# Sample chunks of two token mixers in column and row tiles, placed by 0/1 matrices, with four weight blocks moved between state updates

## The reference, cut to what matters

```python
def gdn_chunk(S, inp):            # S: (B, H, dk, dv)
    ...
    v_new = value - jnp.einsum('bhld,bhdv->bhlv', kcd, S)
    o = jnp.einsum('bhld,bhdv->bhlv', q * jnp.exp(G)[..., None], S) + jnp.einsum('bhtj,bhjv->bhtv', qk, v_new)
    S_new = S * jnp.exp(GL)[..., None] + jnp.einsum('bhjd,bhjv->bhdv', k * jnp.exp(GL - G)[..., None], v_new)
def gla_chunk(S, inp):
    ...
    o = jnp.einsum('bhtc,bhcv->bhtv', q * jnp.exp(Bc), S) + jnp.einsum('bhtj,bhjv->bhtv', A, v)
    S_new = S * jnp.swapaxes(jnp.exp(BL), -1, -2) + jnp.einsum('bhjc,bhjv->bhcv', k * jnp.exp(BL - Bc), v)
```

## Time and profile before

| | us |
|---|---|
| median of 3 runs (lowest, highest) | 993.27 (988.12, 995.01) |
| the profiled execution, its own time | 989.5 |
| its span, first to last instruction | 987.8 |
| chunk 2 of stage two from its first product with old states (267.83) to the start of stage three's blocks (344.22) | 76.4 |
| blocks 0 to 7 of stage three, to the last copy's start (379.96) | 35.7 |
| chunk 2 of stage three, first update (452.12) to the end of its outputs (487.43) | 35.3 |

### The profile page before, as it was taken

One profiled execution on the slowest core, in us unless ns is written; L12 is line 12 of the kernel. 1 busy time (PEld: TensorE's weight loads), 2 busy tenths in 40 slices (PEclk: granted clock), 3 DMA queues, 4 the chain that ended last, 5 costly groups with the idle time before them and its releaser, 6 DMA issues. The chain is left out here.

```text
span 987.8 us, 16585 instructions
## 1 busy us (share of the span) xinstructions
PE 911.3 (92%) x7010; PEld 775.9 (79%) x7010; DVE 421.3 (43%) x714; ACT 296.8 (30%) x595; POOL 222.2 (22%) x242
## 2 busy tenths in 40 slices
PE   8999989997999699999978999999899999999993
PEld 7988868886998589868848999999898666665551
DVE  5787854445313533053165643167234222222223
ACT  6775553230112325131036544423211000000003
POOL 8411326554241000000043400575400000000000
PEclk9999999997697699997559999999989999999998
DMA  9934024000002494401066455444059999999992
GB/s 241 291 98 127 1 54 131 1 1 1 2 1 86 137 311 129 128 10 43 1 215 182 131 169 170 143 157 159 13 175 375 423 422 420 421 421 418 422 410 65
DMA packets 97895, 175.41 MB, mean 178 GB/s; under 512 B 9012, under 2 KB 84372, under 8 KB 85477
## 3 DMA queue, kind: packets, MB, share of 16 engines
q1 hardware_dynamic: 97816, 174.29, 49.4%
HBM read 163.13 MB, written 10.95 MB: 176 GB/s over the span
## 5 line engine op out<-in xcount | busy, mean ns | idle before, releaser
L272 PE MATMUL ps<-rounded,rounded 128*128 128x304 f32 x632 | 197.3, 312 | 13.5 <-DVE rounded L260 9.5
L274 PE MATMUL ps<-rounded,rounded 128*128 128x304 f32 x632 | 192.6, 305 | 0.0
L273 PE MATMUL ps<-hL,rounded 128*128 128x304 f32 x504 | 153.9, 305 | 0.0
L272 PEld LDWEIGHTS ps<-rounded,rounded 128*128 128x128 f32 x632 | 120.8, 191 | 24.9 <-DVE rounded L260 9.7
L274 PEld LDWEIGHTS ps<-rounded,rounded 128*128 128x128 f32 x632 | 120.9, 191 | 0.0
L260 DVE TENSOR_TENSOR rounded<-ring,rounded 128x2048 fp32r<-128x2048 f32 x36 | 83.8, 2328 | 71.5 <-ACT rounded L254 70.9
L254 ACT ACTIVATE rounded<-ring 128x2048 fp32r<-128x2048 f32 x48 | 91.2, 1909 | 27.8 <-PE ps L274 16.2
L273 PEld LDWEIGHTS ps<-hL,rounded 128*128 128x128 f32 x504 | 97.0, 192 | 0.4 <-issue 0.2
L260 POOL TENSOR_TENSOR rounded<-ring,rounded 128x2048 fp32r<-128x2048 f32 x12 | 55.3, 4606 | 89.4 <-ACT rounded L254 89.2
L1085 PE MATMUL ps<-arena 128*128 128x128 f32 (+1 forms) x576 | 64.6, 277 | 1.7 <-DVE arena L1005 1.3
L1085 PEld LDWEIGHTS ps<-arena 128*128 128x128 f32 (+1 forms) x576 | 62.1, 191 | 3.2 <-DVE arena L1005 1.9
(11 more groups left out here) (378 smaller groups left out, 1716.7 us busy)
## 6 DMA issues: line engine op xcount, KB each, us to landing
ring<-in_w_in SPq DMA_DIRECT2D x36, 1024.0 KB, 5.8
ring<-in_expert_w_gate SPq DMA_DIRECT2D x16, 1024.0 KB, 20.7
ring<-in_expert_w_up SPq DMA_DIRECT2D x16, 1024.0 KB, 15.8
ring<-in_expert_w_down SPq DMA_DIRECT2D x16, 1024.0 KB, 23.5
arena<-in_expert_w_down SPq DMA_DIRECT2D x12, 1024.0 KB, 21.0
arena<-in_expert_w_gate SPq DMA_DIRECT2D x12, 1024.0 KB, 21.4
arena<-in_expert_w_up SPq DMA_DIRECT2D x12, 1024.0 KB, 24.4
ring<-in_w_proj_a SPq DMA_DIRECT2D x4, 1024.0 KB, 5.1
```

The costliest lines, as they stand in the source:

```text
L272: self.nc.tensor.matmul(self.psum[b][:, 0:NT], h[:, j, c], xh(j), start=(j == 0), stop=False)
L273: self.nc.tensor.matmul(self.psum[b][:, 0:NT], h[:, j, c], xl(j), start=False, stop=False)
L274: ins = self.nc.tensor.matmul(self.psum[b][:, 0:NT], lo[:, j, c], xh(j), start=False, stop=(j == KB - 1))
```

## The change

In stage two, chunk 2:

- The queries and the keys of the same token of a sample are put side by side (`both`, in unused columns of `bEG`): 8 weight columns per sample. `old_states` now makes 8 matmuls per head, one for each sample, with the state streamed (128 columns) and results at partitions 32g to 32g+8, g = 0 to 3. So four samples lie in four column tiles. ACT and DVE copy the results out (`OLD`), and matmuls with 0/1 matrices (`PLACE`, `ROWS`) put the rows where the 48-token matrix wants them. The segment masks and the masked copies of keys and queries are gone.
- For the updates, keys (`KR`, by 16 DMAs within SBUF) and new values (`VR`, by `rows` and two copies per half) lie at partitions 32g to 32g+4. A matmul contracts 4 rows. POOL multiplies the states by their decay ahead of it, and DVE adds 512 columns at a time.
- Outputs are accumulated directly with channels in rows (four matmuls per head), so that the transposes go.
- Blocks 0 to 3 of stage three run between the four rounds of updates. ACT, DVE and POOL split their weights there (`HQ`, two buffers in ring slots 2 and 3).

In stage three, blocks 4 to 7 remain at the start; value weights are loaded later where they would overwrite `HQ`; in chunk 2 the old states are streamed against 4 query columns in column tiles before the updates, copied out by ACT and placed with `PLACE`. In stage one, POOL builds `PLACE` and `ROWS` in place of four masks (`GM`).

The diff, cut to its core:

```diff
@@ front, POOL
-        link(nc.gpsimd.tensor_tensor(GM[:, 0, :], U, BLK, ALU.mult))
-        for r, m in ((1, 64), (2, 32), (3, 16)):
...
+        link(nc.gpsimd.memset(k.places, 0.0))
+        for x in range(2):
+            for w in range(2):
+                v = k.PLACE[w][x][:, TAIL + 16 * x:TAIL + 16 * x + 16]
+                link(nc.gpsimd.memset(v, 1.0))
...
+                keep(v, [[-32, 4], [-1, TS]], -4 * w, 1)
+                keep(v, [[32, 4], [1, TS]], 4 * w, -1)
@@ delta, SP
+        for hh in range(2):
+            sp.wait_ge(s["p9_done"], 5 + hh)
+            for x in range(2):
+                for g in range(4):
+                    at = TAIL + TS * (4 * x + g)
+                    sp.dma_start(KR[hh][x][32 * g:32 * g + TS, :, :], Kd[at:at + TS, 2, 4 * hh:4 * hh + 4, :]).then_inc(s[f"kr{hh}_in"], 16)
@@ delta, POOL (c == 2)
-                    nc.gpsimd.tensor_tensor(SEGM[:, h, :, :], bc_mid(KT[:, h, 256:NT], 9), MT[:, :, :], ALU.mult).then_inc(s["ktm_ready"], 1)
+                    nc.gpsimd.tensor_copy(both(hh)[:, :, :, 1, :], KT[:, hs, TP:NT].rearrange("p h (b t) -> p h b t", t=TS)).then_inc(s["kc_ready"], 1)
...
+                    pl.wait_ge(s["old_done"], h // 4 + 1)
+                    st = sample_state(h)
+                    nc.gpsimd.tensor_tensor(st, st, bc_last(egl3[:, 1:9, h], 128), ALU.mult).then_inc(s["decayed"], 1)
+                    if h == 3:
+                        core.low_part(pl, nc.gpsimd, N_QB + 1, core.HQ, core.HQ[1])
+                for n in range(N_QB + 2, N_QB + 4):
+                    core.low_part(pl, nc.gpsimd, n, core.HQ, core.HQ[n % 2])
@@ delta, ACT (c == 2)
+                core.high_part(act, N_QB, core.HQ, core.HQ[0])
+                for hh in range(2):
+                    act.wait_ge(s["old_done"], hh + 1)
+                    nc.scalar.activation(OLD[hh][0], bank4(4 * hh + 2), ACT.Copy).then_inc(s["old0_ready"], 1)
+                core.high_part(act, N_QB + 1, core.HQ, core.HQ[1])
...
+                for b in range(4):
+                    act.wait_ge(unit_done, blocks_before + b + 1)
+                    nc.scalar.activation(QK[:, b, :], psum[4 + b][:, 0:NT], ACT.Copy, scale=128 ** -0.5).then_inc(s["qk_ready"], 1)
+                    if b % 2:
+                        core.high_part(act, N_QB + 2 + b // 2, core.HQ, core.HQ[b // 2])
@@ delta, DVE (c == 2)
+                for r in range(4):
+                    dve.wait_ge(s["decayed"], 2 * r + 2)
+                    for g in range(4):
+                        dve.wait_ge(s["su_done"], 4 * r + g + 1)
+                        st = (SA if r < 2 else SB)[:, 2 * (r % 2):2 * (r % 2) + 2, g::4, :]
+                        nc.vector.tensor_tensor(st, st, psum[g][:, :].rearrange("p (h x v) -> p h x v", h=2, x=2), ALU.add).then_inc(s["su_ready"], 1)
+                    if r == 0:
+                        prompt_state(0)
+                        prompt_state(1)
@@ delta, PE (c == 2)
+                def old_states(hh):
...
+                    for h in range(4):
+                        for x in range(2):
+                            for g in range(4):
+                                ins = mm(bank4(4 * hh + 2 + x)[32 * g:32 * g + 8, h, :], buf[hh][bEG][:, h, 64 + 8 * (4 * x + g):72 + 8 * (4 * x + g)],
+                                         sample_state(4 * hh + h)[:, 4 * x + g, :], start=True, stop=True)
+                def old_values(hh):
+                    o = psum[4 * hh][0:l, :]
+                    mm(o, PLACE[1][0], OLD[hh][0], start=True, stop=False)
+                    for h in range(4):
+                        mm(bank4(4 * hh)[0:TAIL, h, :], KT[:, 4 * hh + h, 256:TP], S[:, 4 * hh + h, :], start=False, stop=False)
+                    mm(o, PLACE[1][1], OLD[hh][1], start=False, stop=True).then_inc(s["ks_done"], 1)
+                def rows(hh):
+                    mm(psum[4 * hh + 3][:, :], ROWS[0], buf[hh][bDT][0:l, :, :], start=True, stop=True).then_inc(s["row0_done"], 1)
+                    mm(psum[4 * hh][:, :], ROWS[1], buf[hh][bDT][0:l, :, :], start=True, stop=True).then_inc(s["row1_done"], 1)
+                def updates(r):
+                    hh = r // 2
+                    for g in range(4):
+                        if r:
+                            pe.wait_ge(s["su_ready"], 4 * (r - 1) + g + 1)
+                        for n in range(4):
+                            h, x = 2 * (r % 2) + n // 2, n % 2
+                            ins = mm(bank4(g)[:, n, :], KR[hh][x][32 * g:32 * g + TS, h, :], VR[hh][x][32 * g:32 * g + TS, h, :], start=True, stop=True)
+                        ins.then_inc(s["su_done"], 1)
+                old_states(0); old_states(1); old_values(0); old_values(1)
+                values(0); values(1); rows(0); rows(1)
...
+                updates(0)
+                for h in range(8):
+                    mm(o[:, h, :], OLD[hh][0][:, q, :], PLACE[0][0], start=True, stop=False)
+                    mm(o[:, h, :], OLD[hh][1][:, q, :], PLACE[0][1], start=False, stop=False)
+                    mm(o[:, h, 0:TAIL], S[:, h, :], buf[hh][bEG][:, q, 0:TAIL], start=False, stop=False)
+                    ins = mm(o[:, h, :], buf[hh][bDT][0:l, q, :], buf[hh][bAT][0:l, q, 0:l], start=False, stop=True)
...
+                next_block(0); updates(1); next_block(1); updates(2); next_block(2); updates(3); next_block(3)
@@ gla, PE
-        for b in range(8):
+        for b in range(4, 8):
...
+        for h in range(HB):
+            for x in range(2):
+                for g in range(4):
+                    t = slice(TAIL + TS * (4 * x + g), TAIL + TS * (4 * x + g) + TS)
+                    ins = mm(psum[OB[h]][32 * g:32 * g + TS, 256 * x:256 * x + 256], Q2[:, h, 0, t], SS[h][:, 4 * x + g, :], start=True, stop=True)
+            ins.then_inc(s["old_done"], 1)
...
-                for b in range(8):
-                    t = slice(TAIL + TS * b, TAIL + TS * b + TS)
-                    ins = mm(o2[:, h, e, t], SS[h][:, b, v], Q2[:, h, 0, t], start=False, stop=(b == 7))
+                for x in range(2):
+                    ins = mm(o2[:, h, e, :], OLD[h][:, 256 * x + 128 * e:256 * x + 128 * e + 128], PLACE[0][x], start=False, stop=(x == 1))
```

More of the change, by code:

```diff
@@ L830, in delta, with both @@
     (bDT, bB, bD0, bB0, bD2, bB2, bD, bE, bY, bAT, bEG) = range(11)
-    KDM = [[k.carve(MB[hh] + 512 * (2 + 3 * x), 9 * 128, 9, 128) for x in range(2)] for hh in range(2)]
+    KR = [[buf[hh][bD0], buf[hh][bB0]] for hh in range(2)]
+    VR = [[buf[hh][bD2], buf[hh][bD]] for hh in range(2)]
+    OLD = [[buf[hh][bB], buf[hh][bB2]] for hh in range(2)]
+    QK = k.carve(0, 8 * NT, 8, NT)
+    blocks_before = units(N_QB)
+    def both(hh):
+        return buf[hh][bEG][:, :, 64:128].rearrange("p h (b w t) -> p h b w t", w=2, t=TS)
     SA = k.carve(A1 + 11264, 4096, 4, 8, 128)
@@ L986, in _ @@
+            if c < 2:
+                for hh in range(2):
+                    i, b0 = 2 * c + hh, 4 * hh
+                    act.wait_ge(s["o_done"], i + 1)
+                    nc.scalar.activation(oaT[:, 4 * hh:4 * hh + 4, T0[c]:T0[c] + l], bank4(b0 + 2, l), ACT.Copy).then_inc(s["oT_ready"], 1)
     @block.vector
@@ L1055, in _ @@
             else:
+                core.low_part(dve, nc.vector, N_QB, core.HQ, core.HQ[0])
+                for hh in range(2):
+                    dve.wait_ge(s["old_done"], hh + 1)
+                    nc.vector.tensor_copy(OLD[hh][1], bank4(4 * hh + 3)).then_inc(s["old1_ready"], 1)
                 residual(0)
@@ L1189, in _ @@
             else:
-                def old_states(b, hh, stop):
+                def old_states(hh):
+                    pe.wait_ge(s["y4_ready"], 5 + hh)
+                    pe.wait_ge(s["qe_ready"], 5 + hh)
+                    pe.wait_ge(s["kc_ready"], 1 + hh)
                     for h in range(4):
-                        for q in range(9):
-                            st = S[:, 4 * hh + h, :] if q == 0 else sample_state(4 * hh + h)[:, q - 1, :]
-                            ins = mm(bank4(b, 128)[0:l, h, :], SEGM[:, 4 * hh + h, q, :], st, start=(q == 0), stop=(stop and q == 8))
-                        if not stop:
-                            ins = mm(bank4(b, 128)[0:l, h, :], buf[hh][bAT][0:l, h, 0:l], buf[hh][bDT][0:l, h, :], start=False, stop=True)
-                    return ins
@@ L1237, in delta @@
+                next_block(1)
+                pe.wait_ge(s["kr1_in"], 16 * 8)
+                updates(2)
+                pe.wait_ge(s["oT_ready"], 5)
+                next_block(2)
+                updates(3)
+                pe.wait_ge(s["s_ready"], 6)
+                next_block(3)
     ctx.close()
@@ L1371, in _ @@
         link = Chain(dve, s["dve_c"])
-        for n in range(N_QB, N_Z - 1):
-            k.low_part(dve, nc.vector, n, HI)
+        for n in range(N_VB, N_Z - 1):
+            k.low_part(dve, nc.vector, n, HI, HI[n % 3])
         for c in range(3):
@@ L1467, in _ @@
             if u < 4:
[L1468 removed]
```

(1 more changed line is left out.)

214 lines of the change are left out of this document (94 added, 120 removed).

## The result

The changed kernel takes 962.9 us (median of four runs, 958.4 to 967.5) beside 990.7 us for the kernel before: a ratio of 0.973, 95% interval 0.969 to 0.977, so 27.8 us less. The profiled execution took 963.0 us.

What follows compares the result with a forecast made beforehand. The end was taken to hang on a chain through PE and the expert-weight stream: 989.5 less 7.2 (stage two) and 16.9 (stage three) gives 965.4, or 967 with half the median's offset; range 941 to 988 us.

Steps and rivals of the forecast that it cites:

- rows: Stage two, on PE: eight instructions of 512 columns, 3.9 us at full clock, 7.2 at half; 3.9 taken.
- three rounds with blocks: Stage two: three rounds of update and block, 7.3 us each at full clock, 13.3 at half; 8.4 each taken, 25.2.
- changes of shape: Stage two, on PE: about ten changes of tile shape cost between 0 and 3.3 us; 2 taken.
- end, PE without work: Stage two after block 3: ACT's copies and high part, POOL's last low part, the hand-over; PE idle 8.5 us.
- stage three, chunk 2: Old states 3.6, update 1.15, outputs 12.6, changes of shape 1: 18.4 us against 35.3, so 16.9 less.
- what stands beside this at no cost: Stage two: POOL's eight decays (18 us) and two earlier low parts (9 us) run beside PE's work without lengthening it.
- a new wait of PE for V's weights or POOL's decays: A sign in the changed profile that would make the forecast wrong; no size given.
- No overlap between row tiles: Stage two's first round: 32 instructions, four in a row on the same rows, no overlap: 3.9 us full, 7.2 half.
- Outputs bound by the clock: Stage two: 64 output instructions take 14.2 us at half clock, 7.1 at full; 14.2 taken.
- Rival 2: Both stretches: the clock holds, as busy PE and blocks in between keep it; 942.7 us, chance 0.20.
- Rival 4: Old states of stages two and three: column tiles of 8 and 4 columns don't overlap; 987.1 us, chance 0.08.
- Rivals 3 and 5: 3: clock stays half through rounds of stage two, 998.2 us, chance 0.07; 5: waits between take both gains back, 989, 0.05.

Runs made afterwards that it cites:

- control: The changed kernel with no edit, timed again as the level for the other runs: 964.1 us, ratio 0.974 to the kernel before.
- low_late: Changed kernel with the second weight slot's low part moved from POOL to DVE, after the first round's additions: 961.9 us, 0.973 of the kernel before.
- upd_inner: Changed kernel with each round's sixteen update products issued with the row tile changing at each: 950.9 us, 0.960 of the kernel before.
- clock_blocks: Changed kernel with block 0 ahead of the outputs, block 1 in their middle, blocks 2 and 3 behind rounds two and three: 964.4 us, 0.973 of the kernel before.
- blocks_last: Changed kernel with blocks 0 to 3 put behind all four rounds of updates: 967.0 us, 0.977 of the kernel before.

## Why the prediction was right, and where its terms were off

The mechanism was that of the forecast: both stretches shrink, the expert stream moves forward with them, and the clock comes and goes in the rounds. Predicted were 7.2 + 16.9 = 24.1 us off the profiled time; 26.5 were measured. By terms, in us (one profile; the old states take 4.6 to 6.2 us in the ten profiles that have them, by where the clock rises within them):

| Term | Predicted | Measured |
|---|---|---|
| old states | 5.9 | 4.6 |
| placing them | 5.8 | 5.8 |
| residual and new values | 3.0 | 7.6, of it 4.6 of waiting |
| rows | 3.9 (7.2 at half) | 7.1 |
| first round | 5.5 | 5.1 |
| outputs | 14.2 | 15.8 |
| prompt state | 3.6 | 3.7 |
| block 0 | 5.0 | 5.2 |
| three rounds with blocks | 25.2 | 20.5 |
| changes of shape | 2.0 | within the other terms |
| end, PE without work | 8.5 | 8.0 |
| sum | 82.6 | 83.3 |
| block 4 behind the pause | 2.7 | 2.1 |
| stage three, chunk 2 | 18.4 | 19.3 |

- **The step that failed** is "what stands beside this at no cost: POOL's eight decays and its two earlier low parts". It counted POOL's time and not whom POOL holds up. The low part beside DVE's residual cost PE 4.6 us (3.7 in control), and low_late took most of it away. The prediction did name "a new wait of PE for V's weights or POOL's decays" as a sign of being wrong; the wait that came stands behind POOL's low part, by way of DVE, and no term had a price for it.
- **Rows** were priced at the full clock, on the view that the clock falls in the first round; it fell at 282.1, in the wait ahead of the new values of half 1, so that the rows stood at half throughout. That is the other bound which the text gave. With the wait down to 1.18 us it fell within the rows all the same, as low_late showed.
- **The rounds** were priced too high: 6.3, 7.8 and 6.3 us with their blocks, 4.7 us less in all. Rounds two to four found the full clock (2.82, 3.06 and 2.81 us), since a block ahead of them had brought it back, and are cheaper there than the 3.9 us that were counted: 3.0 us of the 4.7. A change of shape shows as a start some 0.09 us late (0.23 us from the start of block 0's last matmul to that of round two at 321.21, within the block 0.14); by this one, ten would be about 1 us, an estimate. The rounds, the changes and the old states pay for the wait, the rows and the outputs. That the sum came so close is luck: errors of up to 4.7 us, of both signs, met in it.
- **Stage three** has the same in small: its old states take 3.6 us as priced, its outputs 14.6 and not 12.6, with six of the eight groups at 2.0 us, and its 1 us for changes of shape does not show.
- **No overlap between row tiles** was nearly right for this order of the statements: within the four products of one tile the records start 0.111 us apart at the full clock, one after the other, and only at the three changes of tile does the next tile's first one start ahead of the last ones (at 321.76, the last at 322.09). So a round took 2.82 us and not the 3.9 that were counted, and 5.1 and not 7.2 at the low clock. upd_inner shows what it was a property of: the order. The prediction took it as given and so did not see 9 us.
- **Outputs bound by the clock**: clock_blocks had them in 9.8 us. The sentence holds; that an order with blocks between them would save time does not.
- **Rival 2** (the clock holds) would have needed outputs near 7 us; PE was busy for 5.00 of 5.00 us from 300 to 305 at 0.50. The rule of the Trainium skill (TensorE: Matmul & The Clock Gate, "Why this matters for your kernels") weighed in the prediction, that matmuls without idle gaps keep the full clock, speaks for that rival. The fall at 282.1 comes behind a gap of 4.62 us, as that rule has it; but PE was then busy throughout from 284 to 315 and the clock stayed at 0.50, so that the trace differs from it once more. **Rival 4** fell: 64 old-state records of 8 columns take 1.92 us at the full clock, 0.030 each, as column tiles that overlap do. **Rivals 3 and 5** fell by the rounds and by the end.
- The end came out as written: ACT's part, POOL's 4.49 us, the hand-over, 7.98 us without work on PE.

## What to carry to other kernels

Work that is put on an idle engine is only free if no instruction of another engine that someone waits for needs what it holds: look for operations with two SBUF operands on DVE beside each long one on POOL. Where matmuls use small tiles of the array, let neighbours in the order lie in different tiles; that was worth more here than any moving of blocks. And where the clock is low in a stretch, an order that helps one step can take it from the next, as here: compare the mean clock and the length of the whole stretch before counting a gain.

## What the runs showed of the hardware

- **DVE's additions of two SBUF operands and POOL's instructions shut each other out.** In all twelve profiles the residual met a POOL instruction in both halves, and ended 0.54 to 0.55 us after that one did: 282.39 after 281.85 in the changed kernel, 276.93 after 276.39 in low_late. Where DVE came first, POOL paid: of the four decays beside half 0 one takes 2.36 us instead of 1.91 (least, median and most in ns):

```profile
L940 POOL TENSOR_TENSOR arena<-arena,small x4: 1912/1912/2359, 269.4 to 275.0; 128x1024 f32<-128x1024 f32 x4
```

  DVE's additions of a PSUM operand beside a low part keep their 0.6 to 0.7 us (four in 2.53 us from 328.76 on, POOL's part from 329.91). The Trainium skill (SBUF — State Buffer, "Who interferes with whom") says this: a DVE instruction with two SBUF inputs and a GpSimd instruction that reads SBUF exclude one another, and the order of issue decides who waits. The trace agrees, with 4.81 against 0.86 us.
- **Row tiles overlapped only between neighbours in the order.** 16 products of 4 rows take 2.82 us with four in a row in one tile and 1.17 with the tile changing at each; at the low clock 5.13 and 2.09. (The bank changes with the tile; see upd_inner.) The Trainium skill (TensorEngine Tiling (Array Packing), "Key Properties") says that different tiles work in parallel; the runs agree, with 1.17 us, and add that the order decides it.
- **No order tried here bought a higher clock.** The mean over some 60 us was 0.64 and 0.66 for two orders of the same work, with the same time, though the outputs ran 6 us faster in one. With all blocks behind the updates (blocks_last, 281.4 to 343.1) it was 0.60, and the stretch 2.8 us longer than in control, so an order can lose time. Why the clock falls at 280 to 282 us stays open: in control PE was waiting, in low_late it had waited for 1.18 us and then been busy for 1.3 us with operands of 48 rows.
